# A decoder layer on one core: the output projection split by the halves of its inner dimension

## What is computed

```
x = x + 0.5 * swiglu_1(rmsnorm(x))
h = rmsnorm(x);  proj = h @ w_in
y_a = rmsnorm_per_head(attend(q_a, k_a, v_a, logf))        # 8 attention heads, paged cache for the samples
h_m, C, n, m = mlstm(q_m, k_m, v_m, i, f, C0, n0, m0)      # 8 recurrent heads
y_m = sigmoid(o_m) * rmsnorm_per_head(h_m)
x = x + concat([y_a, y_m]) @ w_out                         # inner dimension 2048: 1024 of y_a, 1024 of y_m
x = x + 0.5 * swiglu_2(rmsnorm(x))
```

## Time and profile before

| | us |
|---|---|
| median of 3 runs | 2371.96 (2370.81 to 2373.31) |
| the profiled execution, its own time | 2367.73 |
| its span in the profile | 2366.1 |
| PE busy | 2299.5, 97% of the span |
| DVE busy | 1220.3 |
| ACT busy | 841.8 |
| mean granted clock of PE | 0.987 |

### The profile page before, as it was taken

How to read it: one execution, slowest core, us unless ns; L and a number is a source line. 1 busy time by engine, 2 the same in 40 slices (tenths; PEclk the granted TensorE clock), 3 DMA queues, 4 the chain that set the end, 5 groups by cost and what they waited for, 6 DMA issues and landing times.

```text
span 2366.1 us, 47910 instructions
## 1 busy us (share of the span) xinstructions
PE 2299.5 (97%) x17725; PEld 2244.9 (95%) x17725; DVE 1220.3 (52%) x1873; ACT 841.8 (36%) x1098; POOL 48.6 (2%) x81
## 2 busy tenths in 40 slices
PE   7999999999999999987999979999999999999998
PEld 6999999999999999875999859999999999999998
DVE  6555544354454465565347764564455344555443
ACT  4333333333333343342234422443333333333332
POOL 2000000000000010000000110000000000000000
PEclk9999999999999999998999979999999999999999
DMA  5555555555555444556454533455555555555553
GB/s 154 177 170 165 161 169 169 169 168 169 167 160 169 167 153 134 174 187 201 136 166 160 159 104 124 151 174 170 164 162 169 166 171 167 171 165 160 169 168 129
DMA packets 175661, 383.91 MB, mean 162 GB/s; under 512 B 18949, under 2 KB 44669, under 8 KB 175245
## 3 DMA queue, kind: packets, MB, share of 16 engines
q1 hardware_dynamic: 172736, 375.98, 50.3%
q0 software_dynamic: 2432, 5.57, 0.7%
q10 hardware_dynamic: 416, 1.32, 0.2%
HBM read 373.09 MB, written 9.70 MB: 162 GB/s over the span
## 4 chain that ended last, share of the span: by engine, by line
PE 93%; DVE 4%; ACT 1%; issue 1%; DMA 1%; ACTq 0%; POOL 0%; DVEq 0%; SPq 0%; POOLq 0%
PE ps L1555 29%; PE ps L1553 29%; PE ps L1554 29%; DVE w_lo L905 1%; PE ps L1641 1%; PE ps L1782 1%; PE ps L1795 0%; ACT w_hi L580 0%; DVE C L1470 0%; DVE w_raw L1470 0%; DMA x_rows<-in_x_sample 0%; DVE xt L931 0%; DVE sq L922 0%; PE ps L1853 0%; PE ps L1611 0%
## 5 line engine op out<-in xcount | busy, mean ns | idle before, releaser
L905 DVE TENSOR_TENSOR w_lo<-w_raw,w_hi 128x1024 fp32r<-128x1024 f32 (+1 forms) x690 | 788.8, 1185 | 1025.4 <-ACT w_hi L580 1023.9
L580 ACT CAST w_hi<-w_raw 128x1024 fp32r<-128x1024 f32 (+1 forms) x690 | 669.4, 1017 | 1308.5 <-PE ps L1555 1305.4
L1553 PE MATMUL ps<-x_hi,w_hi 128*128 128x288 f32 (+1 forms) x2752 | 812.4, 295 | 5.0 <-DVE w_lo L905 3.2
L1555 PE MATMUL ps<-x_hi,w_lo 128*128 128x288 f32 (+1 forms) x2752 | 814.7, 296 | 0.0
L1554 PE MATMUL ps<-x_lo,w_hi 128*128 128x288 f32 (+1 forms) x2752 | 808.3, 294 | 0.0
L1553 PEld LDWEIGHTS ps<-x_hi,w_hi 128*128 128x128 f32 x2752 | 518.4, 188 | 6.1 <-DVE w_lo L905 3.3
L1554 PEld LDWEIGHTS ps<-x_lo,w_hi 128*128 128x128 f32 x2752 | 522.1, 190 | 0.1
L1555 PEld LDWEIGHTS ps<-x_hi,w_lo 128*128 128x128 f32 x2752 | 517.5, 188 | 0.0
L1555 PE MATMUL ps<-hid_hi,w_lo 128*128 (+1 forms) x1376 | 406.8, 296 | 0.0
L1553 PE MATMUL ps<-hid_hi,w_hi 128*128 (+1 forms) x1376 | 405.3, 295 | 1.4 <-DVE X L1080 1.4
L1554 PE MATMUL ps<-hid_lo,w_hi 128*128 (+1 forms) x1376 | 403.6, 293 | 0.0
(11 more groups left out here) (452 smaller groups left out, 1345.0 us busy)
## 6 DMA issues: line engine op xcount, KB each, us to landing
w_raw<-in_w_down SPq DMA_DIRECT2D x178, 512.0 KB
w_raw<-in_w_gate SPq DMA_DIRECT2D x320, 256.0 KB
w_raw<-in_w_up SPq DMA_DIRECT2D x320, 256.0 KB
w_raw<-in_w_in SPq DMA_DIRECT2D x64, 512.0 KB
w_raw<-in_w_in SPq DMA_DIRECT2D x64, 384.0 KB
w_raw<-in_w_out SPq DMA_DIRECT2D x32, 512.0 KB
page<-in_cache_k SPq DMA_DIRECT2D x16, 512.0 KB, 3.8
w_raw<-in_w_gate SPq DMA_DIRECT2D x32, 192.0 KB
```

Of the source, the lines that this page charges most:

```text
L580: nc.scalar.copy(w_hi[:, slot, 0:width], w_raw[:, slot, 0:width]).then_inc(w_hi_ready, 1)
L905: nc.vector.tensor_tensor(w_lo[:, slot, 0:width], w_raw[:, slot, 0:width], w_hi[:, slot, 0:width].bitcast(F32), ALU.subtract).then_inc(w_l ...
L1553: mm(out, hi, x_hi[:, k, :], start=first and pair == 0 and s == slots[0], stop=False)
L1555: ins = mm(out, lo, x_hi[:, k, :], start=False, stop=last and pair == 1 and s == slots[-1])
```

## The change

"out" becomes three kinds of groups: out_a (one group, 6 tiles, 768 columns) and out_b (two groups, 5 tiles, 640 columns each), which multiply attention's half of the inner dimension (8 slots, two turns each), and out_m (two groups, 8 tiles), which multiplies the recurrent half. Half of X is added after each of them (out_add and residual). A **step** is one pair: 0 to 3 are out_a, 4 to 11 out_b, 12 to 19 out_m.

- Attention's squares and their sums, mean and root move to before and into in_m. The root is spread in the loop over the heads, through the unused half of bank 2, and ya_hi and ya_lo are made there, in the memory of heads' ext that is no longer read. The samples' share is spread once before the loop.
- The counts of the samples move ahead of the last state_out; the two transposes follow the samples' numerators at once, and then out_a begins.
- The sums of counts and of the samples' squares stand after the last tile of step 0. The chain of reciprocals and the root of the recurrent heads (8 rows of 288, no longer 576) lies between DVE's splits of steps 2 to 6; the spreads stand in steps 5, 6, 8 and 9.
- The copies of the stored state into ext move ahead of DVE's wait for the row exponentials.
- The products of the out phase are written out, where "out" was a loop.

The diff, cut to what the prediction speaks of:

```diff
...
-    mixer = [("in_a", 4, KD, KD, plain[:6]), ("in_m", 4, KD, KD, plain), ("out", 2, KD, KD, plain)]
+    mixer = [("in_a", 4, KD, KD, plain[:6]), ("in_m", 4, KD, KD, plain),
+             ("out_a", 1, H, H, plain[:6]), ("out_b", 2, H, H, plain[:5]), ("out_m", 2, H, H, plain)]
...
         with scope:
-            ext = l_("ext", [P, 2 * H, EXTW])
+            l_("ext_offset", [P, 16])
+            ext, ext_r = twin("left", l_, "ext", [P, 2 * H, 320])
...
-            nR_parts = R_all_r, b_all_r
...
+        def load_out():
+
+
+            a, b, m = OUT_A, OUT_B, OUT_M
+            load_turn(a.turn, range(SLOTS), columns(wo, 0, a.width))
+            load_turn(a.turn + 1, range(2), lambda s: columns(wo, 0, a.width)(SLOTS + s))
+            state_traffic()
+            load_turn(a.turn + 1, range(2, SLOTS), lambda s: columns(wo, 0, a.width)(SLOTS + s))
+            with sp.Fori(0, 2) as i:
+                for kt in range(b.turns):
+                    load_turn(i * b.turns + (b.turn + kt), range(SLOTS),
+                              lambda s: columns(wo, i * b.width + a.width, b.width)(kt * SLOTS + s))
+            with sp.Fori(0, 2) as i:
+                for kt in range(m.turns):
+                    load_turn(i * m.turns + (m.turn + kt), range(SLOTS),
+                              lambda s: columns(wo, i * m.width, m.width)(H + kt * SLOTS + s))
 
...
+            turn = step // 2
+            split_pair(OUT_A.turn + turn, step % 2 * 2, out_width(turn) if turn < 10 else groups["gu1c"].width)
+
+        def ya_operand_hi(h):
+
+            act.wait_ge(sem("ya_scaled"), 1 + h + 1)
+            nc.scalar.copy(ya_hi[:, h, :], ya[:, h, :]).then_inc(sem("xn_hi"), 1)
...
+        def ym_operand_hi(h):
+
+            act.wait_ge(sem("ym_scaled"), h + 1)
+            nc.scalar.copy(ym_hi[:, h, :], vm[:, h, :]).then_inc(sem("xn_hi"), 1)
...
+        act.wait_ge(sem("ya_ready"), H + 1)
+        for j in range(H):
+            square(SUM_Y + j, ya[:, j, :])
...
+        sqrt(3, xt[0:H, 0, :], rs[0:H, 0, :])
...
+            if h >= 1:
+                ya_operand_hi(h - 1)
+        ya_operand_hi(H - 1)
...
+        split_out(2)
+        split_out(3)
+        sqrt(4, sq[0:H, 0, :], xt[0:H, 1, :])
+        for step in range(4, 20):
+            split_out(step)
+            if step == 6:
+                ym_operand_hi(0)
+                ym_operand_hi(1)
+            if step == 8:
+                ym_operand_hi(2)
...
+            if step == 17:
+                early_x(range(0, 2))
+            if step == 18:
+                early_x(range(2, 5))
+            if step == 19:
+                early_x(range(5, EARLY))
+        split_out(20)
+        split_out(21)
...
+            dve.wait_ge(sem("sq_ready"), SUM_M + h + 1)
+            nc.vector.scalar_tensor_tensor(ya[:, h, 0:TP], ya[:, h, 0:TP], vecs[:, V_GA + h:V_GA + h + 1],
+                                           ps[:, 2, TP:2 * TP], ALU.mult, ALU.mult).then_inc(sem("ya_scaled"), 1)
+
+        def ya_operand_lo(h):
+
+            dve.wait_ge(sem("xn_hi"), 32 + h + 1)
+            nc.vector.tensor_tensor(ya_lo[:, h, :], ya[:, h, :], ya_hi[:, h, :].bitcast(F32),
                                     ALU.subtract).then_inc(sem("xn_ready"), 1)
+
+        def ym_scale(h):
+
+            dve.wait_ge(sem("ym_spread"), h + 1)
+            nc.vector.scalar_tensor_tensor(vm[:, h, :], vm[:, h, :], vecs[:, V_GM + h:V_GM + h + 1],
+                                           ps[:, 6 + h % 2, 0:T], ALU.mult, ALU.mult).then_inc(sem("ym_scaled"), 1)
+
+        def ym_operand_lo(h):
+
+            dve.wait_ge(sem("xn_hi"), 32 + H + h + 1)
+            nc.vector.tensor_tensor(ym_lo[:, h, :], vm[:, h, :], ym_hi[:, h, :].bitcast(F32),
+                                    ALU.subtract).then_inc(sem("xn_ready"), 1)
+
+        def out_add(g, i, tile):
+
...
+            n = len(g.tiles)
...
+                wait_bank(dve, g, g.turn + i * g.turns, g.index + i, b)
+                x = X[:, tile + b, :]
+                nc.vector.tensor_tensor(x, ps[:, b, 0:T], x, ALU.add).then_inc(banks_free, 1 if b < n - 1 else NBANK + 1 - n)
+
+        def early_x(tiles):
...
+        dve.wait_ge(sem("sum_done"), SUM_Y + H)
+        nc.vector.tensor_scalar(rs[0:H, 0, :], ps[0:H, 2, 0:T], 1.0 / HD, EPS, ALU.mult, ALU.add).then_inc(sem("mean_ready"), 1)
...
+        dve.wait_ge(sem("edges_done"), 2)
+        nc.vector.tensor_copy(n0T[:, :], ps[:, 0, 0:NB * H])
+        nc.vector.tensor_copy(
+            ext[:, :, EXT:EXTW].rearrange("p j (b r) -> p j b r", r=EXTS)[:, :, :, 0:CW - 1],
+            ps[:, 5, 0:384].rearrange("p (j b r) -> p j b r", j=2 * H, b=NB)).then_inc(sem("ext_edges"), 1)
         dve.wait_ge(sem("rows_exp"), 4)
         nc.vector.tensor_copy(s_rows[:, 1, :], nR_row[:, TP:T])
...
         parts(nR_row[:, :], *(x[0:H, :] for x in nR_parts))
...
+        y, tmp, v = xt[0:H, 0, :], xt[0:H, 1, :], rs[0:H, 0, :]
+        dve.wait_ge(sem("sqrt_ready"), 3 + 1)
+        link(nc.vector.reciprocal(y, y))
+        link(nc.vector.tensor_tensor(tmp, y, y, ALU.mult))
+        link(nc.vector.scalar_tensor_tensor(tmp, v, -0.5, tmp, ALU.mult, ALU.mult))
+        link(nc.vector.scalar_tensor_tensor(y, tmp, 1.5, y, ALU.add, ALU.mult))
+        parts(y, *(x[0:H, :] for x in ya_root_parts)).then_inc(sem("root_ready"), 1)
+        nc.vector.tensor_tensor(ya[:, :, TP:T], ya[:, :, TP:T],
+                                vecs[:, V_GA:V_GA + H].unsqueeze(2).to_broadcast([P, H, SM]), ALU.mult)
...
+        dve.wait_ge(sem("ya_spread"), 1)
+        nc.vector.tensor_tensor(ya[:, :, TP:T], ya[:, :, TP:T], ps[:, 2, TP:2 * TP].rearrange("p (h s) -> p h s", h=H),
+                                ALU.mult).then_inc(sem("ya_scaled"), 1)
...
+            ya_scale(h)
+            if h >= 1:
+                ya_operand_lo(h - 1)
+        ya_operand_lo(H - 1)
+
+        dve.wait_ge(sem("nT_done"), 1)
+        nc.vector.tensor_copy(vm[:, :, TP:T], ps[:, 6, 0:256].rearrange("p (h s) -> p h s", h=H)).then_inc(sem("h_sample"), 1)
+        nc.vector.tensor_copy(n_rows[:, 0, :], ps[0:NB * H, 6, 256:256 + HD]).then_inc(sem("n_rows_ready"), 1)
+        nc.vector.tensor_copy(n_rows[0:H, 1, :], ps[0:H, 6, 256 + HD:512]).then_inc(sem("n_rows_ready"), 1)
         nc.vector.tensor_copy(counts[0:SM, :], ps[0:SM, 7, 0:TP])
...
+        split_out(2)
         dve.wait_ge(sem("counts_summed"), 1)
...
+            ins = nc.vector.tensor_tensor(xt[0:H, 0, c], sum_h, r_row[:, c], ALU.mult)
+        link(ins)
+        y, tmp, v = sq[0:H, 0, :], sq[0:H, 1, :], xt[0:H, 1, :]
+        nc.vector.tensor_scalar(v, xt[0:H, 0, :], 1.0 / HD, EPS, ALU.mult, ALU.add).then_inc(sem("mean_ready"), 1)
+        split_out(3)
+        dve.wait_ge(sem("sqrt_ready"), 4 + 1)
+        link(nc.vector.reciprocal(y, y))
+        split_out(4)
+        out_add(OUT_A, 0, 0)
+        split_out(5)
+        link(nc.vector.tensor_tensor(tmp, y, y, ALU.mult))
+        link(nc.vector.scalar_tensor_tensor(tmp, v, -0.5, tmp, ALU.mult, ALU.mult))
+        link(nc.vector.scalar_tensor_tensor(y, tmp, 1.5, y, ALU.add, ALU.mult))
+        link(nc.vector.tensor_tensor(y, y, ws_row[:, :], ALU.mult))
+        parts(y, *(x[0:H, :] for x in ym_root_parts)).then_inc(sem("root_ready"), 1)
+        split_out(6)
+        dve.wait_ge(sem("gated"), H + 1)
+        ym_scale(0)
+        ym_scale(1)
+        split_out(7)
+        ym_scale(2)
+        ym_scale(3)
+        ym_operand_lo(0)
+        ym_operand_lo(1)
+        split_out(8)
+        out_add(OUT_B, 0, 6)
+        split_out(9)
+        ym_scale(4)
+        ym_scale(5)
...
+        split_out(12)
+        out_add(OUT_B, 1, 11)
+        for step in range(13, 17):
+            split_out(step)
+        residual(OUT_M, 0, 1.0)
+        split_out(17)
+        early_x(range(0, 2))
+        split_out(18)
+        early_x(range(2, 5))
+        split_out(19)
+        early_x(range(5, EARLY))
+        split_out(20)
+        residual(OUT_M, 1, 1.0)
+        split_out(21)
         for b in range(4):
...
-        link(nc.vector.tensor_tensor(root[:, 1, :], root[:, 1, :], ws_row[:, :], ALU.mult))
-        parts(root, *root_parts).then_inc(sem("root_ready"), 1)
...
-        first_half(groups["out"], 1.0)
-        last_half(2, groups["out"], 1.0, groups["gu1c"].width)
...
+        head_sums(SUM_Y, 2, range(H))
...
+        pe.wait_ge(sem("mean_ready"), 3 + 1)
...
+        pe.wait_ge(sem("root_ready"), 2)
+        for h in range(H):
+            ins = spread_row(ps[:, 2, TP + h * SM:TP + (h + 1) * SM], h, [x[:, TP:T] for x in ya_root_parts])
+        ins.then_inc(sem("ya_spread"), 1)
...
+            pe.wait_ge(sem("ya_scaled"), 1 + h)
+            spread_row(ps[:, 2, TP:2 * TP], h, [x[:, 0:TP] for x in ya_root_parts])
...
+        pe.wait_ge(sem("qn_ready"), 1)
+        for h in range(H):
+            mm(ps[0:SM, 7, TP:TP + SM], one_hot[:, h, :], qn[:, h, :], stop=True, **add)
+        for h in range(H):
```

(61 more changed lines are left out.)

158 lines of the change are left out of this document (59 added, 99 removed).

## The result

The changed kernel takes 2350.44 us (median of 4 runs, 2346.98 to 2351.99); the kernel before, run beside it, 2371.43 (2370.81 to 2373.31). The ratio is 0.9914, 95% interval 0.9902 to 0.9926: about 21 us less, where 28.3 were forecast. The forecast of 2343.7 is 6.7 us too low; the time lies inside the range of 2338 to 2352. The profiled execution took 2346.98, with a span of 2345.4.

A forecast was written before the change was run, and what follows sets the result against it. PE, busy for 97% of the span, was taken to bound the kernel. The terms -34.8 + 3.5 + 1.8 + 2.3 - 1.1 = -28.3 us, from 2371.96, gave 2343.7 us (2341 to 2347), range 2338 to 2352.

The forecast's parts named there:

- The stretch before the projection: From the last head's state to the output projection: of 40.9 us only 6.1 stay on the path, -34.8 us.
- The out phase: Output projection: sums at full clock 1.4 us and 16 spreading products 2.1 us added to PE's stream, +3.5 us.
- the ramp: PE's clock rising from half at the start of the output projection: costs 2.7 us, left as before.
- rival (a): PE's clock does not fall before in_m or out_a: 4 to 7 us less, 2337 to 2340; chance 0.13.
- (b): DVE and ACT fall behind in the output projection, or several zeros fail: 3 to 8 us, 2347 to 2352; chance 0.23.
- (c): Small products between big ones keep the clock at half through the output projection: 98 us, giving 2442; chance 0.02.
- the zero for the elementwise work: DVE and ACT work beside the output projection's products costs nothing; DVE's sum is 27 of 32 us.
- Rival (d): Program order or an unread bank holds out_a until the roots are there: 34.8 us not gained, 2375; chance 0.02.
- The loop: Loop over the heads: one uncovered wait behind ACT's sigmoid in head 1 delays head 2's state updates, +2.3 us once.
- The sharing of ports: DVE's y_lo and POOL's gating in the heads could wait for each other, 0.73 us in 7 heads; 0.3 us more.
- The preparation: Before the loop over the heads: 16 spreading products of 32 columns, 0.11 us each, +1.8 us (bounds 0.5 and 3.6).
- From attention to in_m: End of attention to in_m's start: DVE's copies no longer wait for ACT's exponentials, -1.1 us (bounds +0.5 and -2).

The follow-up runs named there:

- one-spread: Against the kernel with the sigmoid ahead of the loop: one float32 product spreads all samples' roots instead of 16 small ones; 2340.35 us, ratio 0.9868.

## Why the prediction held, and where it was off

**The stretch before the projection** (-34.8; measured -36.6). Nothing else held the first product, as argued: the work kept is the two numerator groups and two transposes. The surplus of 1.8 is mostly the clock. The forecast had L2158 at half clock like L2000, 3.55; it took 2.31, 1.24 less. The rest is 0.1 each in L2156 and in the transposes, and the first product's overlap of 0.4.

**The out phase** (+3.5; +3.4). Sums 1.67 for 1.4, the spreads some 0.133 each as forecast. The agreement is partly luck: the ramp, left at 2.7 us, cost half of 2.3 (clock 0.50 until 1402), 1.5 less, which is half of rival (a). Against it stands about 1 us that no single record shows: with the half clock taken out, the out phase took 106.2 us after and 101.4 before, 4.8 more, and sums and spreads are 3.8 of that. In the second profile of the changed kernel the ramp was back, and the out phase took 108.7, +4.7. (By the forecast's own rows, all at half clock would have been 2.9 + 4.2 = 7.1 and not 6.7; nothing hung on it.) No stretch of it has PE idle: 105.05 busy of 105.10 us from 1402 on:

```profile
1402.00:1507.10 105.10, 105.05 (x797) 103.78 (x797) 69.86 (x116) 42.50 (x64) 0.88 (x2) 1.00 0.50 154
```

(PE, PEld, DVE, ACT and POOL, then the clock.) So rivals (b) and (c) fall: the zero for the elementwise work holds, with up to 9 us of cover for DVE, and small products between large ones left the clock at 1.00. Rival (d) falls with the gap.

**The loop** (+2.3; +8.4) is the step that failed. The wait itself was sized right: 2.6 us in the head where it was expected, of which the formula had 2.3. The rest the forecast had at zero. By the intervals: half clock between heads 0 and 1, 6.42 - 4.85 = 1.6, gone without the 16 small spreads; half clock in the two heads behind the wait, 1.1 + 1.9 = 3.0, gone with the wait in both kernels that moved the sigmoid; 0.11 in each of seven heads, 0.8, gone where the spreads leave the loop; 0.4 at the end, where the samples' counts stand, which the forecast had at 0 with 1.2 as its bound. Together 8.4. The claim "the state updates of head 2 late by 2 us and no others" was wrong in its second half: the forecast watched the clock at the starts of in_m and of the projection alone, and took the loop's full clock as given. It also read PE's gap of 0.55 off a weight load (PEld in the earlier trace rows). PE itself, over four heads of before, was idle for 0.24 us by its records, 0.06 a head (us, PE busy (instructions), PE clock, DMA share, GB/s):

```profile
1356.52:1375.49 18.97, 18.73 (x193) 1.00 0.91 252
```

So there was hardly a gap for 0.22 of spreads, and half of them showed.

**The sharing of ports.** Every y_lo of the loop that ran beside POOL's gating was longer, e.g. (timelines of POOL and DVE, after):

```profile
1380.79 0.73 POOL L568 TENSOR_TENSOR vm<-vm,om 128x256 f32<-128x256 f32 x1 [4.12 <-ACT sq L900]
```

```profile
1381.14 0.69 DVE L1016 TENSOR_TENSOR ext_r<-ya,ext_r 128x288 fp32r<-128x288 f32 x1
1382.58 2.15 DVE L1587 SCALAR_TENSOR_TENSOR C<-C,s_all,ps 128x128 f32<-128x128 f32 x8 [0.75 <-PE ps L2128]
```

The same instruction took 0.44 us at its shortest, and here it ended 0.31 us after POOL's (1381.83 against 1381.52), while POOL kept its 0.73 of before. So the one that started second waited, which is what the Trainium skill says (page "SBUF — State Buffer", section "SBUF: two separate sides"); the trace agrees, but the price was 0.24 a head and not 0.73, because only 0.38 us of POOL's instruction were left when DVE's began (1381.52 - 1381.14). In the one place where POOL's began second, at 1364.74 beside the y_lo of 1364.32, POOL's took 0.93 us. DVE idled 0.75 behind it, so it cost nothing in these heads, as the forecast had it.

**The preparation** (+1.8; +3.4). The spreads cost 1.8. Nearly all of the other 1.6 is 24 transposes of the recurrent heads' v at the end of in_m (groups by line, busy us, mean ns; after, then one-spread):

```profile
L1885 PE MATMUL ps<-ident,vm 128*128 128x128 f32 (+1 forms) x24 | 4.3, 361 | 0.0
```

```profile
L1886 PE MATMUL ps<-ident,vm 128*128 128x128 f32 (+1 forms) x24 | 2.8, 275 | 0.0
```

They were at half clock where in_m was short (203.9 to 205.4 us) and at full clock where it was long (206.1 to 206.6: both profiles of the kernel before and the first of one spread). PE at in_m's start in the same two kernels (us, PE busy (instructions), PE clock, DMA share, GB/s; after, then one-spread):

```profile
1126.00:1129.00 3.00, 2.22 (x16) 1.00 0.03 5
```

```profile
1125.00:1131.00 6.00, 5.22 (x22) 0.50 0.01 3
```

What joins in_m's length to the clock behind it was not tried. in_m and the preparation together grew by 1.2 us in the first profile, less than the spreads alone, so the half clock there cost that execution nothing; in the second profile of the changed kernel they grew by 2.4 to 2.8.

**From attention to in_m** (-1.1; about 0). The mechanism was there: in_m's start no longer waits for the exponentials. But the sums took 4.0 us instead of 2.9. The forecast took the 4.50 us of L2020 in the earlier trace rows for half clock and halved them, and let ACT's squares set the pace. In fact the clock was up again 1 us after their start, and in the changed kernel PE was busy with them all the time at full clock (PE, before, then after):

```profile
1394.90:1398.40 3.50, 3.46 (x14) 0.99 0.03 6
```

```profile
1119.60:1123.70 4.10, 4.10 (x19) 1.00 0.01 0
```

The gates' products ahead of them ran until 1119.7, 3.4 us after attention's last copy began (forecast: 2.3), at a clock of 0.54 from 1116 to 1119. And behind the mean DVE still had 1.6 us of row work ahead of the copies (1124.14 to 1125.71 in the chain), which the forecast did not count. in_m itself began at clock 1.00 in this profile, without a ramp: the other half of rival (a), and the -2.2 in the table's row of in_m.

## What to carry to other kernels

Price a wait on PE by the clock, too: a wait that made one head 2.6 us longer cost some 5.6 us, since the two heads behind it ran at half clock and took 3.0 more. When work is put into a loop that two engines close, look for the one long instruction that stands in the new work's way on a third engine (here the sigmoid) and move that first; it was two lines. Sixteen products of 32 columns in a row were dear twice, in themselves (1.8 us) and in the half clock behind them (1.6): one product over all columns, with a block-diagonal operand made on an idle engine, gave back 2.7 us of preparation and loop in three of four profiles. In the fourth it was 4.3, with the transposes at full clock.
